# Up-projected queries and keys of latent attention multiplied straight into transposed layout

## The reference

```python
hq, hf, hi, hg, cq, ckv, kr, gate_a, gate_b = jnp.split(h @ w_in, split_idx, axis=-1)
...
q_m = (rmsnorm(cq, g_q_lora) @ w_uq).reshape(B, S, MLA_HEADS, QK_DIM)
q_nope, q_rope = jnp.split(q_m, [QK_NOPE], axis=-1)
kv = (rmsnorm(ckv, g_kv_lora) @ w_ukv).reshape(B, S, MLA_HEADS, QK_NOPE + V_DIM)
k_nope, v_m = jnp.split(kv, [QK_NOPE], axis=-1)
q_full = jnp.concatenate([q_nope, apply_rope(q_rope, ...)], axis=-1)
k_full = jnp.concatenate([k_nope, broadcast(apply_rope(kr, ...))], axis=-1)
att = causal_block_attention(q_full, k_full, v_m)
```

## Time and profile before

| | us |
|---|---|
| median of 3 runs | 1912.54 (1912.38 to 1912.82) |
| the profiled execution | 1911.41 |
| its span | 1909.6 |
| PE busy in the span | 1829.0 (96%) |
| DVE busy | 1295.6 (68%) |
| ACT busy | 891.2 (47%) |
| POOL busy | 107.5 (6%) |

### The profile page before, as it was taken

One profiled execution on the slowest core, in us unless ns is written; L12 is line 12 of the kernel. 1 busy time (PEld: TensorE's weight loads), 2 busy tenths in 40 slices (PEclk: granted clock), 3 DMA queues, 4 the chain that ended last, 5 costly groups with the idle time before them and its releaser, 6 DMA issues.

```text
span 1909.6 us, 24440 instructions
## 1 busy us (share of the span) xinstructions
PE 1829.0 (96%) x8884; PEld 1534.5 (80%) x8884; DVE 1295.6 (68%) x1361; ACT 891.2 (47%) x1007; POOL 107.5 (6%) x76
## 2 busy tenths in 40 slices
PE   1999999999999999999999997999999999999997
PEld 1777888888888888887878886888888888888886
DVE  5898767676676676667767645566666666665557
ACT  4544455654644644653433445434434443443443
POOL 0000000130130130130000001000000000000000
PEclk9999999999999999999999998999999999999999
DMA  9997557655755655646887653666666666665553
GB/s 380 366 346 258 189 176 254 238 181 190 240 176 195 233 176 199 210 164 217 278 287 263 220 190 109 232 229 211 221 226 224 208 233 226 218 216 174 196 188 132
DMA packets 115985, 423.38 MB, mean 222 GB/s; under 512 B 13008, under 2 KB 13392, under 8 KB 115408
## 3 DMA queue, kind: packets, MB, share of 16 engines
q1 hardware_dynamic: 115920, 422.51, 64.8%
HBM read 420.36 MB, written 2.10 MB: 221 GB/s over the span
## 4 chain that ended last, share of the span: by engine, by line
PE 56%; issue 30%; DVE 5%; POOL 5%; DMA 2%; ACT 1%; SPq 0%; POOLq 0%; DVEq 0%; ACTq 0%
PE PS L832 18%; PE PS L833 18%; PE PS L834 18%; DVE ada_acc L1220 3%; POOL dec L196 3%; POOL dec L197 2%; DMA ada_raw<-in_ada 1%; DVE wlo L1213 1%; DMA zT<-in_ada 1%; PE PS L850 1%; PE PS L841 1%; PE PS L1131 0%; DMA raw<-in_w_start 0%; PE PS L867 0%; PE PS L892 0%
## 5 line engine op out<-in xcount | busy, mean ns | idle before, releaser
L1213 DVE TENSOR_TENSOR wlo<-raw,whi 128x1024 fp32r<-128x1024 f32 x600 | 731.8, 1222 | 421.1 <-ACT whi L462 420.9
L462 ACT ACTIVATE whi<-raw 128x1024 fp32r<-128x1024 f32 x600 | 629.6, 1053 | 739.5 <-PE PS L834 663.8
L832 PE MATMUL PS<-whi,hT_hi 128*128 128x512 f32 x1792 | 709.0, 396 | 17.2 <-DVE wlo L1213 9.1
L834 PE MATMUL PS<-whi,hT_lo 128*128 128x512 f32 x1792 | 699.2, 390 | 0.0
L833 PE MATMUL PS<-wlo,hT_hi 128*128 128x512 f32 x1792 | 699.0, 390 | 0.0
L832 PEld LDWEIGHTS PS<-whi,hT_hi 128*128 128x128 f32 x1792 | 337.3, 188 | 89.9 <-issue 8.8
L834 PEld LDWEIGHTS PS<-whi,hT_lo 128*128 128x128 f32 x1792 | 337.2, 188 | 71.5
L833 PEld LDWEIGHTS PS<-wlo,hT_hi 128*128 128x128 f32 x1792 | 337.7, 188 | 67.3 <-issue 0.2
L832 PE MATMUL PS<-whi,cT_hi 128*128 128x512 f32 (+1 forms) x592 | 230.3, 389 | 4.9 <-DVE wlo L1213 3.4
L834 PE MATMUL PS<-whi,cT_lo 128*128 128x512 f32 (+1 forms) x592 | 227.2, 384 | 0.0
L833 PE MATMUL PS<-wlo,cT_hi 128*128 128x512 f32 (+1 forms) x592 | 227.2, 384 | 0.0
(11 more groups left out here) (213 smaller groups left out, 1065.4 us busy)
## 6 DMA issues: line engine op xcount, KB each, us to landing
ada_raw<-in_ada SPq DMA_DIRECT2D x142, 512.0 KB, 4.8
raw<-in_w_gate SPq DMA_DIRECT2D x88, 512.0 KB, 4.2
raw<-in_w_up SPq DMA_DIRECT2D x88, 512.0 KB, 4.2
raw<-in_w_down SPq DMA_DIRECT2D x88, 512.0 KB, 3.8
raw<-in_w_start SPq DMA_DIRECT2D x80, 512.0 KB, 4.6
raw<-in_w_hf SPq DMA_DIRECT2D x32, 512.0 KB, 4.0
raw<-in_w_hq SPq DMA_DIRECT2D x32, 512.0 KB, 5.2
raw<-in_w_hi SPq DMA_DIRECT2D x32, 512.0 KB, 4.1
```

Of the source, the lines that this page charges most:

```text
L462: nc.scalar.activation(whi[:, pl.slot(c), 0:w], raw[:, pl.slot(c), 0:w], ACT.Copy)\
L832: nc.tensor.matmul(o, hi[:, kt, tok], whi[:, s, cols], start=start, stop=False)
L834: last = nc.tensor.matmul(o, lo[:, kt, tok], whi[:, s, cols], start=False, stop=stop)
L1213: nc.vector.tensor_tensor(wlo[:, s, 0:w], raw[:, s, 0:w], whi[:, s, 0:w].bitcast(F32), ALU.subtract)\
```

## The change

The chunks of the no-rope queries and of the latent keys are multiplied the other way round. `multiply_columns` takes a block of 128 by 128 of the weights as stationary operand and the compressed activations of all 256 tokens as the moving one, so that a head's features come out on partitions and its tokens along the bank: 24 matmuls with 256 moving columns a chunk. ACT then copies the pair of banks straight to `qT` (t = 20) and `kT` (t = 22). Both groups of eight transposes, the copies to `stage` and `v` and the later ones from the transposes' banks go. The copy to `qT` waits for `o_summed` of the turn's recurrence, because `attend` reads the first half of `qT`. The waits that stood before the transposes move to the attention scores at t = 27. The condition names the two groups and no turn: it holds in turn 0 and in all three turns of the loop.

```diff
--- before.py
+++ after.py
@@ -605,18 +605,13 @@
             def attention(pl, t, g, back):
 
                 if t == 20:
-                    from_pair(pl, I_UQ, T_UK - 1, stage[:])
+                    if back is not None:
+                        act.wait_ge(sig("o_summed"), back + 1)
+                    from_pair(pl, I_UQ, T_UK - 1, flat(qT))
                 if t == 22:
-                    from_pair(pl, I_UK, T_UR - 1, v[:])
-                if t == 24:
-                    act.wait_ge(sig("q_transposed"), g + 1)
-                    nc.scalar.activation(qT[:], by_tile(XA), ACT.Copy).then_inc(sig("qT_copied"), 1)
+                    from_pair(pl, I_UK, T_UR - 1, flat(kT))
                 if t == 26:
-                    act.wait_ge(sig("k_transposed"), g + 1)
                     from_pair(pl, I_UV, T_HF - 1, v[:])
-                if t == 27:
-                    act.wait_ge(sig("k_transposed"), g + 1)
-                    nc.scalar.activation(kT[:], by_tile(XB), ACT.Copy).then_inc(sig("kT_copied"), 1)
                 if t == 28:
                     act.wait_ge(sig("qr_transposed"), g + 1)
                     nc.scalar.activation(bT[:, 0:HPG], by_tile(XA)[:, 0:HPG], ACT.Copy)\
@@ -834,6 +829,25 @@
                             last = nc.tensor.matmul(o, lo[:, kt, tok], whi[:, s, cols], start=False, stop=stop)
                     last.then_inc(multiplied, 1)
 
+            def multiply_columns(pl, g, c0, c, hi, lo):
+
+                p = pl.pair(g)
+                if c == 0 and not pl.fresh(g):
+                    pe.wait_ge(pair_free[p], pl.freed(g))
+                pe.wait_ge(lo_ready, pl.through(c0 + c))
+                s = pl.slot(c0 + c)
+                for h in range(HPG):
+                    o = PS[:, 2 * p + h // 2, h % 2 * T:(h % 2 + 1) * T]
+                    for k in range(KC):
+                        kt = c * KC + k
+                        cols = slice(k * NW + h * P, k * NW + (h + 1) * P)
+                        start, stop = c == 0 and k == 0 and h % 2 == 0, c == CL - 1 and k == KC - 1
+                        nc.tensor.matmul(o, whi[:, s, cols], hi[:, kt, :], start=start, stop=False, skip_group_check=True)
+                        nc.tensor.matmul(o, whi[:, s, cols], lo[:, kt, :], start=False, stop=False, skip_group_check=True)
+                        last = nc.tensor.matmul(o, wlo[:, s, cols], hi[:, kt, :], start=False, stop=stop,
+                                                skip_group_check=True)
+                last.then_inc(multiplied, 1)
+
             def transpose_group(src, bank):
 
                 for h in range(HPG):
@@ -940,8 +954,11 @@
                     j = i % 2
                     if c == 0:
                         pe.wait_ge(sig("c_low"), j + 1)
-                    multiply(pl, I_UQ + i, CL, T_UQ + i * CL, c, c + 1, cT_hi[:, j], cT_lo[:, j],
-                             NW // 2 if I_UQ + i == I_UR else NW)
+                    if I_UQ + i in (I_UQ, I_UK):
+                        multiply_columns(pl, I_UQ + i, T_UQ + i * CL, c, cT_hi[:, j], cT_lo[:, j])
+                    else:
+                        multiply(pl, I_UQ + i, CL, T_UQ + i * CL, c, c + 1, cT_hi[:, j], cT_lo[:, j],
+                                 NW // 2 if I_UQ + i == I_UR else NW)
                 else:
                     i, c = divmod(t - T_HF, CD)
                     multiply(pl, I_HF + i, CD, T_HF + i * CD, c, c + 1, hT_hi, hT_lo)
@@ -990,16 +1007,6 @@
 
             def attention(pl, t, g, back, total):
 
-                if t == 21:
-                    pe.wait_ge(sig("krT_copied"), 1)
-                    pe.wait_ge(pair_free[pl.pair(I_UQ)], pl.freed(I_UQ) + 1)
-                    transpose_group(stage, XA).then_inc(sig("q_transposed"), 1)
-                if t == 24:
-                    if back is not None:
-                        pe.wait_ge(sig("o_normed"), back + 1)
-                    pe.wait_ge(pair_free[pl.pair(I_UK)], pl.freed(I_UK) + 1)
-                    transpose_group(v, XB).then_inc(sig("k_transposed"), 1)
-                    pe.wait_ge(sig("qT_copied"), g + 1)
                 if t == 25:
                     pe.wait_ge(sig("qr_rotated"), g + 1)
                     for hp in range(HPG // 2):
@@ -1010,7 +1017,11 @@
                     last.then_inc(sig("qr_transposed"), 1)
                 if t == 27:
 
-                    pe.wait_ge(sig("kT_copied"), g + 1)
+                    if back is not None:
+                        pe.wait_ge(sig("o_normed"), back + 1)
+                    pe.wait_ge(sig("krT_copied"), 1)
+                    pe.wait_ge(pair_free[pl.pair(I_UQ)], pl.freed(I_UQ) + 1)
+                    pe.wait_ge(pair_free[pl.pair(I_UK)], pl.freed(I_UK) + 1)
                     pe.wait_ge(sig("qrT_copied"), g + 1)
                     for h in range(HPG):
                         for tt, s, o in ((0, 0, PS[:, XA + h // 2, (h % 2) * 2 * P:][:, 0:P]),
```

## The result

The changed kernel is slower. Its median is 1922.77 us (1921.41 to 1925.07, 4 runs) against 1912.68 (1912.38 to 1913.46, 4 runs) for the kernel before: a ratio of 1.0055, 95% interval 1.0043 to 1.0067. That is 10 us, where 3.5 was forecast, and above the range that was given.

A forecast was written before the change was run, and what follows sets the result against it. PE, busy 96% of the span, was taken as the bound, except where it waits on ACT and DVE. Turn 0 -1.18, loop +2.28 and clock +2.4 gave +3.5 us on 1912.54, so 1916.0 us, range 1911.8 to 1918.5.

The forecast's parts named there:

- Transposes gone, -0.89 us a group: On PE, two groups of eight transposes a turn go, 0.89 us each, 1.78 us a turn.
- -1.18 us of turn 0: Turn 0 on PE: no stall there, so the whole balance counts, 4 x 0.15 - 1.78 = -1.18 us.
- The new form, 0.120 us a matmul: On PE, 24 matmuls of 256 columns at 0.120 us each; a changed chunk takes 0.15 us more.
- The queue on ACT, +1.65 us a turn: Loop turns: the copy waits for `o_summed`, delaying chunk 23 by 1.65 us; its stall grows from 0.97 to about 3.1.
- the term of 2.4 us: Behind chunk 23's longer stall, the granted clock falls in two of three loop turns, 1.2 us each: +2.4 us.
- keys' transposes, three turns: Behind chunk 24 in each loop turn, the keys' transposes on PE are gone: -0.89 us a turn.
- The one with three falls of the clock: Chunks 23 to 25: clock falls in all three loop turns, 1.0 to 1.6 us each; +4.1 to +5.8 in all; 33%.

The follow-up runs named there:

- the kernel of 1907.65 us: Changed kernel with cross scores in `stage`, no wait for the sum before the queries' copy, and 32 idle transposes at TensorE's program start: 1907.65 us, ratio 0.9977.
- the shifted kernel (1917.78 us): Changed kernel with 32 idle transposes (64 instructions) added at the start of TensorE's program: 1917.78 us, ratio 1.0026 against the kernel before.

## Why the prediction was wrong, step by step

- **Transposes gone, -0.89 us a group: right.** In the loop, the stretch from chunk 23 to the attention scores shows them by themselves where the clock doesn't fall: 449.58 to 464.35 in the kernel of 1907.65 us, 14.77 us for 15.66. Turn 0 can be read from the sum up to the first chunk 23 of the loop: PE began turn 0's attention 0.48 us earlier than before (290.52 for 291.00), -1.18 us of turn 0 and +1.65 us of the queue were forecast, together -0.01, and 450.23 for 450.08 is +0.15.
- **The new form, 0.120 us a matmul: right.** 290.52 to 293.39 is 2.87 us for 24, the value of the earlier trace rows.
- **The queue on ACT, +1.65 us a turn: right.** The three turns have +1.74, +1.75 and +1.72, and the stall was 3.23 us for 3.1. Taking the wait away brought it to 1.73 us, and the queries' half alone carries the loss.
- **The clock: it fell, and the term of 2.4 us was too small.** The term is two falls at 1.2 us each, and no run shows it. Behind the stall of 3.66 us the kernel before has eight matmuls in 883.08 to 886.48 at a granted clock of 0.50, 1.6 us more than at 0.23 each. In the changed kernel the clock fell to 0.50 at all three stalls of 3.23 us, not two. In the first turn it stayed down for 6.8 us (449.0 to 455.8), partly in the stall, and cost 2.1 us instead of 1.2; in the other two it was down for 3.4 us and cost 1.0 us each. That is 4.1 us. Where the stall before chunk 23 is 1.73 us it fell in no turn (granted 1.00). In the shifted kernel (1917.78 us) it fell to 0.50 at all three too.
- **What failed is the step that isn't there: the program itself.** I counted the added matmuls as work and not as code. The changed loop crosses seven times in its first turn and so touches an eighth piece of PE's program, and packets come again at the jump back (510.7 and 513.9 us) and in turns 2 and 3. I read it as the head being gone when PE jumps back. That is 1.44 and 1.65 us of stall and a fall of the clock to 0.50 for 3.4 us at each (from 513.85 and from 660.62), and the two jumps with the first chunk behind them cost 3.1 and 3.2 us, 6.3 in all. The sum had no term for it.

| term, us | forecast | in the profiles |
|---|---|---|
| turn 0 | -1.18 | -1.11 |
| queue on ACT, three turns | +4.95 | +5.2 |
| keys' transposes, three turns | -2.67 | -2.67 |
| clock behind chunk 23 | +2.4 | +4.1 |
| the two jumps | none | +6.3 |
| ahead of turn 0 and behind the loop | none | -1.8 |
| sum | +3.5 | +10.0 |

The last term is chance as far as I can tell: PE begins turn 0 0.48 us earlier, and 1.35 us less pass behind the loop, where the stall of 1.84 us at 983.45 doesn't occur in the changed kernel's profile. Without the jumps the forecast terms come to +5.5 us and not +3.5. Placed well, the same change gave a ratio of 1.0026, that is 1917.0 by the ratio and 1917.78 as its median, against the 1916.0 that I predicted. Both are inside the range, and the profile of that kernel has the three falls at 3.9 us instead of 2.4. So the size of the clock's price was wrong as well, but that alone kept the time within the range; the jumps took it out.

What these runs show is that a loop with six crossings in its first turn brings no packet in turns 2 and 3, and one with seven, without a hint, does. By the estimate of 256 instructions a packet that is seven pieces and eight. How much PE keeps, and what makes room for a new piece, no run shows. I hadn't weighed it, and the trace of before could have raised the question: six crossings in its first turn, and none after. That the limit was one piece away it doesn't tell.

- **Rivals.** The one with three falls of the clock (+4.1 to +5.8 us) is what the well placed kernel shows: three falls, 5.0 us by the ratio. None had the jump.

What stays open: how much a fall of the clock costs in one run and the next. The runs of one kernel spread over 1 to 8 us here, and the profiles of one run each show 3.4 or 6.8 us at a granted clock of 0.50 behind stalls of the same length.

## What to carry to other kernels

A change that adds instructions to a loop on an engine can have a cost that no busy time shows, here 6.3 us at two jumps for 64 instructions: count the instruction packets from the loop's first turn on, and see whether any come in the later ones; if they do, place the loop's head or give the jump a hint before judging the change. Ask of a copy that moves into another buffer who still reads that buffer: a wait that is put further forward in an engine's queue delays what stands behind it, here a path of 10 us through ScalarE and VectorE by 1.74 us a turn. And where a change has two halves, time each: here one was worth 4 us (1908.03 against 1912.04) and the other cost 6.6 (1918.82 against 1912.25).

## What the runs showed of the hardware that was not expected

- The same 64 idle instructions ahead of a loop made one kernel 5 us faster (1922.8 to 1917.8) and another 6 to 7 us slower (ratio 1.0031, medians 1912.0 and 1919.2).
- In the five kernels whose packets come again in turns 2 and 3, each of the ten jumps back costs 1.44 to 1.94 us of stall, and nine of the ten came with 3.4 or 6.8 us at a granted clock of 0.50, beginning up to 1.2 us before the stall ended or up to 0.8 us after. In the changed kernel that doubles the price (1.4 and 1.6 us more).
- A stall of 1.73 us before chunk 23 left the granted clock at 1.00 in all three turns of three kernels, while it fell to 0.50 behind one of 1.44 us at a jump (513.33 us). A stall of 3.66 us that every kernel has between 874 and 897 us came with a fall to 0.50 in thirteen kernels and in the fourteenth (1907.65 us) with none. So the length of a stall alone doesn't say whether the clock falls. Between chunk 23 and the jump, what stands ahead differs: full matmuls, and 1.84 us of matmuls with one moving column (L881). That this is the reason is argued and wasn't tried.
- A hint at the loop's head took the jump's stall from 1.44 and 1.65 us to nothing measurable (branches of 0.26 and 0.22 us for 3.35 and 3.56), at one instruction more.
